# The output projection of a convolution block as three products of rounded and remainder parts, inside a three-layer kernel

## The chip, the cores and the metric

The kernel runs on one core of one Trainium2 chip. The metric is the device time of one launch, in microseconds (us). Engines are named as in the profile: PE is TensorE's matrix multiplication and PEld its weight load, DVE is VectorE, ACT is ScalarE, POOL is GpSimd, SP is SyncE, which here only issues transfers.

## The reference

Three transformer-like layers over 256 tokens of width 1024, all in float32. The middle one is a convolution block, and the change is in its last steps:

```python
def conformer_conv(h, w_in, b_in, dw_w, dw_b, ln_g, ln_b, w_out, b_out):
    val, gate = jnp.split(h @ w_in + b_in, 2, axis=-1)
    u = val * jax.nn.sigmoid(gate)
    u = depthwise_conv_centred(u, dw_w) + dw_b      # 31 taps over the tokens
    u = jax.nn.silu(layer_norm(u, ln_g, ln_b))
    return u @ w_out + b_out                        # w_out is 1024 x 1024
```

A gated feed-forward (`ffn1`) follows it, and then the third layer, which holds a diagonal state-space scan. The scan needs tables that depend on its parameters alone (`a_re`, `a_im`, `log_dt`, `b_re`, `b_im`): exponentials, sines and cosines of angles reduced to one turn. The kernel works them out early, beside the convolution block; this is the scan set-up.

## The kernel before

Everything is kept in SBUF; only weights stream in. They come in chunks through a ring of four slots of 3072 columns (`ring`), in an order fixed in `ORDERED`; SP issues a chunk's load when the last user of the slot's chunk before has signalled. The output weights of the convolution block are four chunks `conf_o` of two 128-row blocks each (2048 columns), so each takes two thirds of a slot. Each engine has its program written out in order; semaphores join them. Activations lie feature by feature: 1024 features are 8 blocks k of 128 partitions, 256 tokens are the columns, in two tiles t of 128.

A float32 product of TensorE is written as one `matmul`, and the trace lists two records for it: the 32 matmuls of `out_rows` are 64 records of line 840. A product of tensors of type fp32r (float32 rounded to what one pass takes) is one record. The feed-forwards already use this: ScalarE rounds each weight block to a high part (`Copy` into fp32r, line 1622), VectorE subtracts it from the weight (low part, line 2221), and TensorE forms high x high, high x low and low x high (lines 894, 895 and 929).

The convolution block, in order:

- TensorE: eight pairs of input products (`glu_pair`, 809), four of the eight channel blocks' convolution as products (`conv_taps`, 1315, and `conv_sum`, 1326, for blocks 4 to 7), the two sums of the layer norm over the features (1350), a broadcast of the gains (`row_bc`, 818), the bias (834), and then `out_rows` (840): for k 0 to 3 both token tiles, for k 4 to 7 first tile 0, then `row_bc(3)`, then tile 1 with four transposes of the next norm (778) in it. After that the first block of `ffn1` (914).
- ScalarE: sigmoid of each gate (`glu_gate`, 1940), copies of what `conv_taps` left in PSUM (`conv_rows`, 1948), `conv_out` (1953), then the squares of the layer norm (1965), a root (1967), eight SiLUs (1970) that write `cout`, and then its part of the scan set-up: two exponentials (1973, 1975) and four sines (1978 to 1982).
- VectorE: `glu_in` (2560) for each block, the 31 taps for blocks 0 to 3 as a chain of 120 `scalar_tensor_tensor` (2574), both of whose tensor inputs lie in SBUF, the layer norm's arithmetic (2587 to 2597), and then the scan set-up (2600 to 2675): `lam_re` ... the two reduced angle arrays `f0`, `f1` (2600 to 2626, its first half) and coefficients and tables (2630 to 2675, its second half). Its end, `bbar_ready`, releases ScalarE to the first rounding for `ffn1`; VectorE goes on with `row_diag(3)` (2185), which TensorE's `row_bc(3)` needs, and with `split` (2221) and `post` (2200 to 2208), the norm and residual after the projection.
- GpSimd: four builds of tap matrices (2936, a `tensor_tensor` of 992 columns) and some clearing, up to 535 us; then nothing until the third layer.

## Time and profile before

| | us |
|---|---|
| median of 3 runs | 1345.48 (1345.28 to 1346.31) |
| span of the profiled execution, first to last instruction | 1342.6 |
| convolution block's projection on TensorE (line 840) | 620.0 to 652.0 |
| busy over the span: PE / DVE / ACT / POOL | 1271.3 / 865.9 / 507.1 / 124.1 |

The profiled execution has no time of its own beside its span in the figures at hand; the median of the runs is 2.9 us above the span. A span counts from the first to the last instruction on the core, so sums over the trace are made against 1342.6 and carried over to 1345.48 with that 2.9 us kept. Times of the trace are in us from the start of the span, durations of single instructions in us or ns as marked.

### The profile page before, as it was taken

The numbers are of one execution on the slowest core, as the hardware profiler recorded it, in microseconds if no ns is written. First come the engines' busy times: TensorE is split into PE (matmuls) and PEld (weight loads), VectorE is DVE, ScalarE is ACT, GpSimd is POOL, SyncE is SP. The second block draws the span as 40 slices with busy tenths as digits, with TensorE's granted clock in tenths as the row PEclk, the third lists the DMA queues.
The fourth block names the chain that finished last, engine by engine and source line by source line (L and its number), as shares of the span: only waits on it lengthen the run. The fifth ranks groups of instructions, "written<-read, shape, count | busy, mean of one in ns | idle before, by whom it ended". The sixth has DMA issues, their size and how long they took to land. (4 is left out here: it accounts for less than half of the span.)

```text
span 1342.6 us, 19019 instructions
## 1 busy us (share of the span) xinstructions
PE 1271.3 (95%) x7198; PEld 985.6 (73%) x7198; DVE 865.9 (64%) x1505; ACT 507.1 (38%) x857; POOL 124.1 (9%) x165
## 2 busy tenths in 40 slices
PE   3999979989999998999999999899999999899997
PEld 1787645554888887874688888687778785688886
DVE  0547886444777775886777776499952432777776
ACT  2664266324544444014644443302123312544443
POOL 0061021000000002000000000255520000000000
PEclk9999989999999998999999999999999999899999
DMA  9322376984655542421555555033324323455551
GB/s 390 128 82 95 134 299 267 386 318 172 218 187 187 189 155 81 148 92 54 190 210 189 188 189 202 33 126 141 141 95 142 112 100 118 161 188 187 188 187 60
DMA packets 24949, 225.78 MB, mean 168 GB/s; under 512 B 2737, under 2 KB 2865, under 8 KB 4658
## 3 DMA queue, kind: packets, MB, share of 16 engines
q1 hardware_dynamic: 23328, 220.31, 45.0%
q10 hardware_dynamic: 1554, 4.56, 1.0%
q8 instruction: 45, 0.74, 0.2%
q14 instruction: 22, 0.18, 0.0%
HBM read 223.81 MB, written 1.05 MB: 167 GB/s over the span
## 5 line engine op out<-in xcount | busy, mean ns | idle before, releaser
L894 PE MATMUL psum<-aT_r,arena_r 128*128 128x512 f32 x920 | 327.7, 398 | 1.5 <-DVE arena_r L2221 1.3
L2221 DVE TENSOR_TENSOR arena_r<-ring,arena_r 128x1024 fp32r<-128x1024 f32 x188 | 220.2, 1220 | 106.5 <-ACT arena_r L1622 106.5
L809 PE MATMUL psum<-aT,ring 128*128 128x256 f32 (+1 forms) x1136 | 265.3, 391 | 0.0
L895 PE MATMUL psum<-aT_r,arena_r 128*128 128x256 f32 x920 | 258.1, 281 | 0.0
L809 PEld LDWEIGHTS psum<-aT,ring 128*128 128x128 f32 x1136 | 214.1, 191 | 45.9 <-issue 18.8
L1622 ACT ACTIVATE arena_r<-ring 128x1024 fp32r<-128x1024 f32 x188 | 186.8, 1051 | 149.8 <-PE psum L929 133.6
L929 PE MATMUL psum<-arena_r 128*128 128x512 f32 x876 | 213.4, 392 | 0.0
L894 PEld LDWEIGHTS psum<-aT_r,arena_r 128*128 128x128 f32 x920 | 172.9, 188 | 44.2 <-issue 2.2
L929 PEld LDWEIGHTS psum<-arena_r 128*128 128x128 f32 x876 | 159.5, 188 | 34.8
L895 PEld LDWEIGHTS psum<-aT_r,arena_r 128*128 128x128 f32 x920 | 173.8, 189 | 2.6
L1634 ACT ACTIVATE nrm<-nrm 128x256 f32<-128x256 f32 x76 | 31.8, 418 | 164.6 <-DVE nrm L2239 161.4
L792 PE MATMUL psum<-ring,cond 128*32 128x384 f32 x512 | 53.7, 545 | 24.7 <-DMA consts<-in_consts 12.7
L2574 DVE SCALAR_TENSOR_TENSOR arena<-arena,cols 128x256 f32<-128x256 f32 x120 | 52.8, 481 | 1.9
L792 PEld LDWEIGHTS psum<-ring,cond 128*32 128x32 f32 x512 | 14.7, 116 | 52.5 <-issue 35.1
L2239 DVE TENSOR_REDUCE nrm<-psum 128x256 f32<-128x512 f32 x73 | 49.8, 682 | 0.0
L2256 DVE TENSOR_TENSOR nrm<-nrm 128x256 f32<-128x256 f32 x76 | 32.3, 426 | 21.7 <-ACT nrm L1634 16.3
L2246 DVE TENSOR_REDUCE nrm<-psum 128x256 f32<-128x512 f32 x42 | 29.0, 691 | 20.8 <-PE psum L895 20.8
L2346 DVE SCALAR_TENSOR_TENSOR arena<-arena,cols 128x512 f32<-128x512 f32 (+1 forms) x48 | 35.3, 763 | 1.1
L2012 ACT ACTIVATE arena<-psum,cols 128x256 f32<-128x256 f32 x24 | 11.4, 473 | 58.2 <-PE psum L809 58.2
L2264 DVE TENSOR_TENSOR arena_r<-nrm,arena_r 128x256 fp32r<-128x256 f32 x73 | 31.1, 425 | 2.5
L840 PE MATMUL psum<-ring,yT 128*128 128x512 f32 x64 | 28.3, 595 | 2.3 <-DVE o L2522 1.4
L1513 PE MATMUL psum<-yT,ring 128*128 128x256 f32 x128 | 29.0, 380 | 0.9 <-DVE yT L2816 0.9
(499 smaller groups left out, 1620.7 us busy)
## 6 DMA issues: line engine op xcount, KB each, us to landing
ring<-in_w_ffn SPq DMA_DIRECT2D x44, 1536.0 KB, 6.6
ring<-in_w_mod SPq DMA_DIRECT2D x32, 1536.0 KB, 8.9
ring<-in_w_ff SPq DMA_DIRECT2D x32, 1024.0 KB, 4.9
ring<-in_w_in_g SPq DMA_DIRECT2D x8, 1536.0 KB, 6.4
ring<-in_w_conf_i SPq DMA_DIRECT2D x8, 1024.0 KB, 4.9
ring<-in_w_hyb_f SPq DMA_DIRECT2D x4, 1536.0 KB, 6.5
ring<-in_w_in_a SPq DMA_DIRECT2D x4, 1536.0 KB, 6.4
ring<-in_w_in_b SPq DMA_DIRECT2D x4, 1536.0 KB, 6.8
```

Of the source, the lines that this page charges most:

```text
L792: last = mm(mod_acc[q:q + 32, :], cond[:, at:at + 32], slot(c)[:, k * MOD_C:(k + 1) * MOD_C], start=(m == m0 and k < 4), stop=(m == m1 - 1 ...
L809: last = mm(bank(use)[:, out_at:out_at + rhs(k).shape[1]], weights[:, k * P:(k + 1) * P], rhs(k), start=(k == 0), stop=(k == KT - 1))
L894: mm(bank(use).rearrange("p (a t) -> p a t", a=2), hi, x_both[:, :, k, :], start=(k == 0), stop=False)
L895: last = mm(bank(use)[:, T:2 * T], lo, x_hi[:, k, :], start=False, stop=(k == KT - 1))
L929: last = mm(Y[:, t, half * 512:half * 512 + 512], act_part, w_part[:, half * 512:half * 512 + 512], start=(isinstance(i, int) and j == 0 a ...
L1622: fn(out_hi[2] if last_out else w_hi[j % 2][:, at], slot(c)[:, at], ACT.Copy).then_inc(split_hi, 1)
L1634: fn(sg[:, j % 2, :], g_sum[:, j % 2, :], func).then_inc(act_on, 1)
L2221: tt(lo, slot(c)[:, at], hi.bitcast(F32), ALU.subtract).then_inc(split_ready, 1)
L2239: summed = v.reduce_sum(g_sum[:, j % 2, :], bank(gate).rearrange("p (a t) -> p t a", a=2), axis=AXX)
L2256: tt(h_tmp, sg[:, j % 2, :], u_sum if parts == 3 else sg[:, j % 2, :], ALU.mult).then_inc(h_step, 1)
L2346: last = stt(cv[:, b, 0:n, :], cin[:, b, 0:n, k:k + T], taps[:, b, k:k + 1], cv[:, b, 0:n, :], ALU.mult, ALU.add)
L2574: last = stt(cc[:, c, :], cu[:, c, k:k + T], dww[:, c, k:k + 1], cc[:, c, :], ALU.mult, ALU.add)
```

## The change

The output projection of the convolution block becomes three fp32r products for each one in float32: `out_rows_parts` takes the place of `out_rows`. For it

- ScalarE rounds the eight weight blocks (`conf_weights`, a `Copy` of 128x1024) between its `glu_gate`, `conv_rows` and `conv_out` steps; the high parts go to the free third of the ring slots and to four other free places;
- GpSimd subtracts each high part from its weight block, in place in the ring (eight `tensor_tensor` of 128x1024, both inputs in SBUF), each as soon as its rounding is done;
- after each SiLU ScalarE rounds `cout` (`conf_round`, 128x256) and VectorE makes the low part (`conf_part`, a subtraction of 128x256);
- the first half of the scan set-up moves: on VectorE from behind the layer norm to ahead of it, on ScalarE the two exponentials and four sines from behind the SiLUs to between the `conv_out` steps and ahead of the squares.

```diff
--- before.py
+++ after.py
@@ -443,6 +443,10 @@
             s = SLOT_OF[c]
             return ring[:, s * SLOT:(s + 1) * SLOT]
+        def out_weights(c, kk, t=None):
+            at = SLOT_OF[c] * SLOT + kk * D
+            return (ring if t is None else t)[:, at:at + D]
+
         def part_of(n, t):
             name, j, at, width = HYB_PARTS[n]
@@ -555,7 +559,11 @@
         taps = [x[:, at:at + D] for x in (yT_t, ybuf_t) for at in (0, D)]
         conv_ev = [view(x, 0, 4, T + 3) for x in (nrm_t, decay_t)]
         Y_quads = psum[:, 2048:4096].rearrange("p (g n) -> p g n", g=4)[:, :, 0:T + 3]
-        cout = csq
+        cout, cout_hi, cout_lo = csq, view(arena_r, 0, KT, T), view(arena_r, 4352, KT, T)
+        spare = [ring_r[:, s * SLOT + 2 * D:s * SLOT + 3 * D] for s in range(SLOTS)]
+        spare = [spare[SLOT_OF[FIRST["conf_o"] + c]] for c in range(4)]
+        conf_o_hi = [spare[0], o_r[:, 0:D], spare[1], arena_r[:, 7168:7168 + D], spare[2], z_r[:, 0:D], spare[3],
+                     arena_r[:, 11264:11264 + D]]
         ring_ready = [sem(f"ring_ready{s}") for s in range(SLOTS)]
@@ -603,6 +611,7 @@
         taps_ready = sem("taps_ready")
         csig_ready, conv31, csq_ready, csq_done = sem("csig_ready"), sem("conv31"), sem("csq_ready"), sem("csq_done")
         ln_sd, ln_x, conf_out = sem("ln_sd"), sem("ln_x"), sem("conf_out")
+        conf_hi, conf_lo, conf_w_hi, conf_w_lo = sem("conf_hi"), sem("conf_lo"), sem("conf_w_hi"), sem("conf_w_lo")
         s5_par, s5_mag, s5_arg, s5_trig = sem("s5_par"), sem("s5_mag"), sem("s5_arg"), sem("s5_trig")
         bbar_ready, logf_in, logf_sp, logf_ready = sem("bbar_ready"), sem("logf_in"), sem("logf_sp"), sem("logf_ready")
         cdiag_ready, s5_tab, masked = sem("cdiag_ready"), sem("s5_tab"), sem("masked")
@@ -622,7 +631,7 @@
         small_trig = view(arena, 14376, 2, S5T, 32)
         glu = view(arena, 15400, 4, P)
         bbd = view(arena, 13352, 2, 4, P)
-        trig_tmp = view(arena, 8232, 6, 512)
+        trig_tmp = view(arena, 8192, 6, 512)
         cdiag = view(arena, 11304, 2, 512)
         y_a, y_b = yT[:, 0:4, :], yT[:, 4:8, :]
         mT = view(tok_t, 0, KT, T)
@@ -865,6 +874,47 @@
                                 norm_tile(p + 2, 0)
                         if t and c == 2:
                             last.then_inc(ring_used, 1)
+                    if t == 0:
+                        last.then_inc(y_first, 1)
+                        row_bc(p + 1)
+                    else:
+                        filled(last, USE["y", p][0])
+
+            def out_rows_parts(c0, p, hi, lo, w_hi_of, act_ready, w_ready, bias=False):
+
+                wait_y(p)
+                if bias:
+                    for t in range(TT):
+                        for half in range(2):
+                            mm(Y[:, t, half * 512:half * 512 + 512], ones[0:1, :],
+                               brow[0:1, half * 512:half * 512 + 512], start=True, stop=False)
+
+                def rows_of(k, t):
+                    w_lo_k = out_weights(c0 + k // 2, k % 2, ring_r)
+                    for n, (act_part, w_part) in enumerate(((hi, w_hi_of[k]), (hi, w_lo_k), (lo, w_hi_of[k]))):
+                        for half in range(2):
+                            last = mm(Y[:, t, half * 512:half * 512 + 512], act_part[:, k, t * P:(t + 1) * P],
+                                      w_part[:, half * 512:half * 512 + 512],
+                                      start=(k == 0 and n == 0 and not bias), stop=(k == KT - 1 and n == 2))
+                    return last
+
+                for k in range(4):
+                    act_ready(k)
+                    w_ready(k)
+                    for t in range(TT):
+                        last = rows_of(k, t)
+                    if k % 2:
+                        last.then_inc(ring_used, 1)
+                for t in range(TT):
+                    for k in range(4, KT):
+                        if t == 0:
+                            act_ready(k)
+                            w_ready(k)
+                        last = rows_of(k, t)
+                        if t and k == 5:
+                            last.then_inc(ring_used, 1)
+                        if t and k == 6:
+                            norm_tile(p + 2, 0)
                     if t == 0:
                         last.then_inc(y_first, 1)
                         row_bc(p + 1)
@@ -1351,7 +1401,8 @@
                 filled(last, use)
             row_bc(2)
             pe.wait_ge(brow_loaded, 16)
-            out_rows(FIRST["conf_o"], cout, 2, lambda k: pe.wait_ge(conf_out, k + 1), True)
+            out_rows_parts(FIRST["conf_o"], 2, cout_hi, cout_lo, conf_o_hi, lambda k: pe.wait_ge(conf_lo, k + 1),
+                           lambda k: pe.wait_ge(conf_w_lo, k + 1), True)
             ffn("ffn1", NF, 3)
@@ -1952,27 +2003,32 @@
                 wait_full(act, use)
                 freed(fn(cc[:, c, :], bank(use)[:, 0:T], ACT.Identity, bias=col("conf_dw_b")[:, c:c + 1]), use)
+            def conf_weights(k):
+
+                c = FIRST["conf_o"] + k // 2
+                act.wait_ge(ring_ready[SLOT_OF[c]], 16 * (TURN_OF[c] + 1))
+                fn(conf_o_hi[k], out_weights(c, k % 2), ACT.Copy).then_inc(conf_w_hi, 1)
+
             for c in range(7):
                 glu_gate(c)
+            for k in range(2):
+                conf_weights(k)
             conv_rows(0)
+            for k in range(2, 6):
+                conf_weights(k)
             glu_gate(7)
-            for n in range(1, len(CONV_PE)):
-                conv_rows(n)
-                conv_out(n - 1)
-            conv_out(len(CONV_PE) - 1)
-            for k in range(KT):
-                act.wait_ge(ln_x, k + 1)
-                fn(csq[:, k, :], cc[:, k, :], ACT.Square).then_inc(csq_done, 1)
-            wait_read(act, USE["ln"][1])
-            fn(crs, crs, ACT.Sqrt).then_inc(ln_sd, 1)
-            for k in range(KT):
-                act.wait_ge(csq_ready, k + 1)
-                fn(cout[:, k, :], csq[:, k, :], ACT.Silu, scale=col("conf_ln_g")[:, k:k + 1],
-                   bias=col("conf_ln_b")[:, k:k + 1]).then_inc(conf_out, 1)
-
+            conv_rows(1)
+            conv_out(0)
+            for k in range(6, KT):
+                conf_weights(k)
+            conv_rows(2)
+            conv_out(1)
             fn(dt, col("log_dt"), ACT.Exp).then_inc(s5_mag, 1)
+            conv_rows(3)
             act.wait_ge(s5_par, 1)
             fn(mag, s5_a, ACT.Exp).then_inc(s5_mag, 1)
+            conv_out(2)
+            conv_out(3)
             act.wait_ge(half_ready, 1)
             act.wait_ge(s5_arg, 1)
             fn(sin_h, phi, ACT.Sin, scale=PI).then_inc(s5_trig, 1)
@@ -1980,6 +2036,24 @@
             act.wait_ge(s5_arg, 2)
             fn(trig_tmp[:, 2, :], trig_tmp[:, 0, :], ACT.Sin, scale=PI).then_inc(s5_trig, 1)
             fn(trig_tmp[:, 3, :], trig_tmp[:, 1, :], ACT.Sin, scale=-PI, bias=halfpi[:, :]).then_inc(s5_trig, 1)
+
+            for k in range(KT):
+                act.wait_ge(ln_x, k + 1)
+                fn(csq[:, k, :], cc[:, k, :], ACT.Square).then_inc(csq_done, 1)
+            wait_read(act, USE["ln"][1])
+            fn(crs, crs, ACT.Sqrt).then_inc(ln_sd, 1)
+
+            def conf_round(k):
+                act.wait_ge(conf_out, k + 1)
+                fn(cout_hi[:, k, :], cout[:, k, :], ACT.Copy).then_inc(conf_hi, 1)
+
+            for k in range(KT):
+                act.wait_ge(csq_ready, k + 1)
+                fn(cout[:, k, :], csq[:, k, :], ACT.Silu, scale=col("conf_ln_g")[:, k:k + 1],
+                   bias=col("conf_ln_b")[:, k:k + 1]).then_inc(conf_out, 1)
+                if k:
+                    conf_round(k - 1)
+            conf_round(KT - 1)
             row_copy(2)
             act.wait_ge(bbar_ready, 1)
             split("ffn1", 0, [2])
@@ -2582,20 +2656,6 @@
                             glu_in(c)
                             break
-            use = USE["ln"][0]
-            wait_full(dve, use)
-            freed(ts(crs, bank(use)[:, 0:T], 1.0 / D, None, ALU.mult), use)
-            wait_read(dve, use)
-            for k in range(KT):
-                tt(cc[:, k, :], cc[:, k, :], crs, ALU.subtract).then_inc(ln_x, 1)
-            use = USE["ln"][1]
-            wait_full(dve, use)
-            freed(mean_eps(crs, bank(use)[:, 0:T], D), use)
-            dve.wait_ge(ln_sd, 1)
-            ch(v.reciprocal(crs, crs))
-            for k in range(KT):
-                tt(csq[:, k, :], cc[:, k, :], crs, ALU.mult).then_inc(csq_ready, 1)
-
             dve.wait_ge(s5_mag, 1)
             ch(ts(lam_re, col("a_re"), -1e-4, None, ALU.min))
             ch.mark(tt(theta, col("a_im"), dt, ALU.mult))
@@ -2624,6 +2684,31 @@
             ch(tt(f0, f0, f5, ALU.subtract))
             ch(tt(f0, f0, f4, ALU.add))
             stt(f1, f0, -1.0, f0, ALU.mult, ALU.max).then_inc(s5_arg, 1)
+
+            use = USE["ln"][0]
+            wait_full(dve, use)
+            freed(ts(crs, bank(use)[:, 0:T], 1.0 / D, None, ALU.mult), use)
+            wait_read(dve, use)
+            for k in range(KT):
+                tt(cc[:, k, :], cc[:, k, :], crs, ALU.subtract).then_inc(ln_x, 1)
+            use = USE["ln"][1]
+            wait_full(dve, use)
+            freed(mean_eps(crs, bank(use)[:, 0:T], D), use)
+            dve.wait_ge(ln_sd, 1)
+            ch(v.reciprocal(crs, crs))
+
+            def conf_part(k):
+
+                dve.wait_ge(conf_hi, k + 1)
+                tt(cout_lo[:, k, :], cout[:, k, :], cout_hi[:, k, :].bitcast(F32), ALU.subtract).then_inc(conf_lo, 1)
+
+            for k in range(KT):
+                tt(csq[:, k, :], cc[:, k, :], crs, ALU.mult).then_inc(csq_ready, 1)
+                if k == 5:
+                    conf_part(0)
+
+            for k in range(1, KT):
+                conf_part(k)
             dve.wait_ge(s5_trig, 2)
             dve.wait_ge(s5_mag, 2)
@@ -2942,6 +3027,12 @@
             ch.sync()
             gp.memset(tick[:, :], 0.0).then_inc(margins, 1)
+            for k in range(KT):
+                pool.wait_ge(conf_w_hi, k + 1)
+                c = FIRST["conf_o"] + k // 2
+                tt(out_weights(c, k % 2, ring_r), out_weights(c, k % 2), conf_o_hi[k].bitcast(F32),
+                   ALU.subtract).then_inc(conf_w_lo, 1)
+
             pool.wait_ge(norm_x, 24)
             ch.mark(gp.memset(cin2[:, :, 0:2], 0.0))
             ch.sync()
```

`conf_weights(k)` stands on ScalarE as: gates 0 to 6, weights 0 and 1, `conv_rows(0)`, weights 2 to 5, gate 7, `conv_rows(1)`, `conv_out(0)`, weights 6 and 7, `conv_rows(2)`, `conv_out(1)`, exponential, `conv_rows(3)`, exponential, `conv_out(2)`, `conv_out(3)`, four sines.

## Rows read from the trace of the kernel before

**Rows 1.** The page: busy time, share of the span, instructions.

```profile
PE 1271.3 (95%) x7198; PEld 985.6 (73%) x7198; DVE 865.9 (64%) x1505; ACT 507.1 (38%) x857; POOL 124.1 (9%) x165
```

**Rows 2.** Timeline of PE: start, us, engine, line, operation, count [idle before <-releaser].

```profile
603.15 1.91 PE L1326 MATMUL psum<-decay,consts 128*32 128x256 f32 x32
605.86 3.69 PE L1350 MATMUL psum<-arena,consts 128*128 128x256 f32 x16 [0.80 <-ACT arena L1953]
611.07 3.69 PE L1350 MATMUL psum<-arena,consts 128*128 128x256 f32 x16 [1.51 <-ACT arena L1965]
614.60 1.88 PE L818 MATMUL psum<-diag,consts 128*128 128x512 f32 x4
...
620.03 22.55 PE L840 MATMUL psum<-ring,arena 128*128 128x512 f32 x48
642.42 1.88 PE L818 MATMUL psum<-diag,consts 128*128 128x512 f32 x4
644.13 5.31 PE L840 MATMUL psum<-ring,arena 128*128 128x512 f32 x12
```

**Rows 3.** Timeline of DVE, the end of the taps, the norm, the set-up.

```profile
587.17 0.48 DVE L2560 SCALAR_TENSOR_TENSOR arena<-psum,cols,arena 128x256 f32<-128x256 f32 x1 [1.78 <-ACT arena L1940]
587.57 14.62 DVE L2574 SCALAR_TENSOR_TENSOR arena<-arena,cols 128x256 f32<-128x256 f32 x32
609.59 0.42 DVE L2587 TENSOR_SCALAR arena<-psum 128x256 f32<-128x256 f32 x1 [7.40 <-PE psum L1350]
...
617.49 2.77 DVE L2597 TENSOR_TENSOR arena<-arena 128x256 f32<-128x256 f32 x8
623.55 0.17 DVE L2600 TENSOR_SCALAR arena<-cols 128x16 f32<-128x16 f32 x1 [3.29 <-ACT arena L1973]
...
629.55 0.69 DVE L2626 SCALAR_TENSOR_TENSOR arena<-arena 128x512 f32<-128x512 f32 x1
...
637.46 1.22 DVE L2185 TENSOR_TENSOR diag<-consts,pcol 128x1024 f32<-128x1024 f32 x1
```

**Rows 4.** Timeline of ACT, places where it is free, and a sine.

```profile
575.86 0.47 ACT L1940 ACTIVATE arena<-psum,cols 128x256 f32<-128x256 f32 x1 [6.43 <-PE psum L809]
579.59 1.03 ACT L1948 ACTIVATE nrm<-psum 128x1036 f32<-128x1036 f32 x1 [3.26 <-PE psum L1315]
...
605.13 0.47 ACT L1953 ACTIVATE arena<-psum,cols 128x256 f32<-128x256 f32 x1 [1.25 <-PE psum L1326]
...
630.27 0.63 ACT L1981 ACTIVATE arena<-arena 128x512 f32<-128x512 f32 x1 [2.59 <-DVE arena L2626]
```

**Rows 5.** The page: a rounding of 128x1024 on ACT.

```profile
L1622 ACT ACTIVATE arena_r<-ring 128x1024 fp32r<-128x1024 f32 x188 | 186.8, 1051 | 149.8 <-PE psum L929 133.6
```

**Rows 6.** Timeline of SP's queue: the loads of conf_o.

```profile
562.04 24.95 SPq L694 DMA_DIRECT2D ring<-in_w_conf_o  x4
```

**Rows 7.** The chain that ended last: three-product rows in a feed-forward.

```profile
1229.19 2.78 PE psum L929 x12
```

**Rows 8.** Timeline of POOL while it builds tap matrices.

```profile
525.23 1.86 POOL L2936 TENSOR_TENSOR yT<-sel,cols 128x992 f32<-128x992 f32 x1
...
527.10 1.86 POOL L2936 TENSOR_TENSOR yT<-sel,cols 128x992 f32<-128x992 f32 x1
...
528.98 2.78 POOL L2936 TENSOR_TENSOR ybuf<-sel,cols 128x992 f32<-128x992 f32 x1
```

**Rows 9.** Timeline of DVE at the same time.

```profile
527.29 2.75 DVE L2185 TENSOR_TENSOR diag<-consts,pcol 128x1024 f32<-128x1024 f32 x1
```

**Rows 10.** That line and the taps of line 2346: duration ns min/median/max.

```profile
L2185 DVE TENSOR_TENSOR diag<-consts,pcol x6: 1217/1222/2748, 230.7 to 1117.5; 128x1024 f32<-128x1024 f32 x6
...
L2346 DVE SCALAR_TENSOR_TENSOR arena<-arena,cols x48: 477/752/1941, 90.2 to 193.3; 128x512 f32<-128x512 f32 x32, 128x256 f32<-128x256 f32 x16
```

**Rows 11.** Timeline of DVE: taps of another layer beside POOL.

```profile
90.25 6.03 DVE L2346 SCALAR_TENSOR_TENSOR arena<-arena,cols 128x512 f32<-128x512 f32 x4
```

**Rows 12.** Timeline of POOL beside those taps.

```profile
91.56 0.90 POOL L2887 TENSOR_TENSOR ring<-ring,rows 128x128 f32<-128x128 f32 x1
92.55 1.90 POOL L2891 TENSOR_TENSOR ring<-ring,consts 128x640 f32<-128x640 f32 x1
```

**Rows 13.** Windows: busy time of PE, PEld, DVE, ACT, POOL, then granted clock.

```profile
621.00:623.00 2.00, 2.00 (x4) 0.92 (x3) 0.00 (x0) 1.98 (x4) 0.00 (x0) 0.50 0.00 0
```

## The prediction

> **What bounds the kernel now.** I read the page first: TensorE is busy for 95% of the span [rows 1], so what counts is time taken from TensorE or waits added to it. Then the timelines of the four engines between 575 and 660 us, the stretch that the change touches, to see who waits for whom there. TensorE ends the channel products at 605.06 (603.15 + 1.91), sums for the layer norm at 605.86 and at 611.07, and from there works without a pause: gains, bias, and the projection from 620.03 [rows 2]. VectorE is idle for 7.4 us before the norm's first instruction at 609.59, because it ended its taps at 602.19 (587.57 + 14.62); it does the scan set-up from 623.55 to 637.4, in the shadow of the projection [rows 3]. So three things set when the projection ends: when VectorE can start the norm (609.59), the chain from there to TensorE's start (10.44 us), and the products. Last I looked at how GpSimd and VectorE behave when both work, because the change puts eight large GpSimd instructions beside the taps.
>
> **The products.** The float32 form: 48 records in 22.39 us up to the start of `row_bc(3)` at 642.42, then 12 records from 644.13 in 5.15 us, 0.429 each [rows 2] (5.15 and not 5.31, since the next instruction starts before the last record ends). 48 at 0.429 would be 20.6; the missing 1.8 us are the clock, granted at 0.50, the lower of its two levels, at 621 to 623 [rows 13], after TensorE's pauses around 605 and 610. The new form has for each (k, t) the same six matmuls as a feed-forward's output rows, 12 of which advance the chain by 2.78 us, 0.232 each [rows 7]. Up to `row_bc(3)` there are 8 pairs for k 0 to 3 and 4 for tile 0: 72 matmuls, 16.7 us in place of 22.39, a gain of **5.7 us** if the clock is at its upper level there. Tile 1 has 24, 5.6 us in place of 16 records at 0.429, 6.9: a gain of 1.3, of which I take **1.0**, since the transposes among them wait for VectorE's norm of tile 0, which gets no faster.
>
> **The start of the projection, taken alone.** SiLU, then rounding, then a subtraction come ahead of the first product. VectorE's norm products begin at 617.49, one per about 0.35 us (8 in 2.77) [rows 3]; the first low part comes behind six of them and costs one more, so it is done at about 620.0, just when TensorE has done the bias. Later blocks need about 0.9 us each on ScalarE (a SiLU and a Copy) and TensorE takes 2.8 us for a block's both tiles, so they are not late. Cost: 0. Without the cover of the bias it would be 1.5 us.
>
> **The roundings of the weights.** Eight Copies at 1.05 us on ScalarE [rows 5]. The loads of `conf_o` are issued from 562.0 to 587.0 [rows 6]. Blocks 0 and 1 fit behind the gate that starts at 575.86 and before `conv_rows(0)` at 579.59 [rows 4]; 2 to 5 between there and the gate that now serves VectorE at 587.17 [rows 3]; the last two after 592.7, when the fourth chunk is in. ScalarE's idle time hides them, cost 0; without it, 8.4 us.
>
> **The moved set-up.** Its first half lasts from 623.55 to 630.24 on VectorE (629.55 + 0.69), 6.7 us [rows 3]. It goes into the 7.4 us of idle time ahead of 609.59, so alone it costs nothing, with 0.7 us to spare. ScalarE's second exponential now waits for VectorE's first set-up values, and `conv_out(2)` and `conv_out(3)` stand behind it, and TensorE's first norm sum behind those: harmless while VectorE ends its taps at 602.2, since `conv_out(3)` can't run before 605.13 anyway [rows 4], but if VectorE is late, they are late with it. The two large sines stand ahead of the squares; they can start only at the end of the half. One is 0.63 us [rows 4]; when the half ends just as the norm starts, they put the first square off by some 0.2. The second half of the set-up (to `row_diag(3)` at 637.46) follows the low parts: 7.2 us after about 15.8 us of norm and parts, so `row_diag(3)` is done some 24 us and the weights' split some 26 us after the norm's start, and tile 0 of the projection ends after 10.5 + 16.7 = 27.2. It is covered, by 1 us for the split.
>
> **GpSimd's subtractions, the disputed part.** Eight `tensor_tensor` of 128x1024 with both inputs in SBUF. The nearest row is one of 992 columns, 1.86 us undisturbed [rows 8], so 1.92 for 1024. The first six are due from 577.4 to 584.5, the last two at about 594, all while VectorE runs its taps, each with two SBUF inputs. What happens then is in three places of the trace. `row_diag` of 1024 columns usually takes 1.22 us [rows 10]; started 0.19 us into a GpSimd `tensor_tensor`, it takes 2.75 [rows 9], 1.53 more, and GpSimd's next one takes 2.78 in place of 1.86 [rows 8]. Four taps of 512 columns, 0.75 each when alone [rows 10], take 6.03 [rows 11], about 3.2 too long, and the GpSimd instructions beside them are long too (a 640-column one 1.90, a 128-column one 0.90) [rows 12]. The two engines take turns, a whole instruction each. Per instruction VectorE loses 1.53 + 0.19 = 1.72 of GpSimd's 1.86; for 1024 columns 1.77. Eight make **14.2 us**, less the 1.78 us that VectorE idled for the gate at 587.17 [rows 3]: the taps end at 602.2 + 12.4 = 614.6. Bounds: at 1.5 us each +10.2, at 2.1 us each +15.0. The Trainium skill (GPSIMD Engine Reference, section Elementwise — side-by-side cycle accounting) gives 4.5 us for a GpSimd add of 2048 columns; that would be an estimated 2.2 us for 1024, and the sum would be about 3 us higher. The trace's 1.86 for 992 speaks against it, though its inputs repeat elements; no row shows two plain inputs of this size.
>
> The Trainium skill (SBUF — State Buffer, section Who interferes with whom) goes a little further than these rows: an instruction of VectorE with two SBUF inputs and one of GpSimd that reads SBUF exclude each other for the whole instruction. By it the price would be 1.92 each, 15.4 in all, and the time 1352.
>
> What is late next: set-up half to 614.6 + 6.7 = 621.3. The second exponential at about 615, two `conv_out` (0.47 each) to 616.1, then TensorE's first sum of 3.7 us; after a pause of 8 to 9 us its clock is likely at the lower level, so it ends at 620 to 622. The norm starts at about 621.5 in place of 609.59: **+11.9**. I add 0.2 for the sines.
>
> **The sum.** +11.9 + 0.2 - 5.7 - 1.0 = **+5.4 us**: span 1348.0, and with the 2.9 us outside it 1350.9, in round numbers 1351.
>
> **The rivals.**
> - *The engines don't get in each other's way here* (or GpSimd yields): the half fits the idle time, and 5.7 + 1.0 are gained, less nothing: 1345.5 - 6.7 = 1338.8. The point from which it decides: the change gains while the taps end before 602.2 + 0.7 + 6.7 = 609.6, that is while VectorE loses under (7.4 + 1.78) / 8 = 1.15 us to each GpSimd instruction. For it: the taps are of 256 columns, unlike any pair in the trace. Against: each of the three places shows whole turns, and 1.15 is under two thirds of 1.86. Chance 0.08.
> - *The loss about equals the gain:* GpSimd takes 0.9 to 1.4 us of VectorE per instruction, or VectorE catches up elsewhere; 1343 to 1348. Chance 0.09.
> - *The forecast,* 1348.3 to 1354. Chance 0.73.
> - *Dearer still:* GpSimd at 2.2 us on plain inputs (+3), or the lower clock again in the norm's second sum and at the projection's start (+1.8 as before): 1354 to 1358. Chance 0.08.
> - *Three products gain nothing over the float32 form,* so that the whole 12.1 stays: 1357.6. The rows of the feed-forward speak clearly against it. Chance 0.02.
>
> **How the numbers follow.** What a measurement of this kernel can tell from no change is about 0.2%, 2.7 us. Slower by more (over 1348.2): the forecast, the dearer case and the one that gains nothing, 0.83. Within: 0.09. Faster by more: 0.08. The range leaves out the first rival and most of the second below, and the last above: 1347 to 1355.5.
>
> **What would show it.** In the changed profile: taps of line 2574 (its new number) of 0.48 us with pauses or lengths of about 2 us wherever a GpSimd `tensor_tensor` of 1024 runs, and the last one ending near 614.6; the norm's first instruction at about 621.5, released by TensorE or following the set-up directly; TensorE idle for some 8 us before its first norm sum; 72 matmuls of the projection in about 16.7 us; no pause of TensorE between bias and projection. The forecast is wrong if the taps still end near 602, if GpSimd's instructions last much under 1.8 us, or if the norm's start is late by less than 7 us.

## The result, and the profile after

The changed kernel takes 1357.08 us (median of 4 runs, 1356.12 to 1357.83), the kernel before 1345.88 beside it (4 runs, 1345.28 to 1346.31): a ratio of 1.0078, 95% interval 1.0065 to 1.0091. It is slower by 11.2 us, where 5.4 were forecast, and 1.6 us above the range. The profiled execution took 1357.83 us, 1.8 more than its span of 1356.0.

The page of the changed kernel, busy time, share of the span and instructions, against [rows 1]: TensorE is no busier, VectorE by 19.5 us, GpSimd by 20.2.

```profile
PE 1271.8 (94%) x7230; PEld 995.4 (73%) x7230; DVE 885.4 (65%) x1513; ACT 516.9 (38%) x873; POOL 144.3 (11%) x173
```

Times of the two traces can't be set side by side as they stand, since this execution is already 2.8 us later when the stretch begins: the gate of block 6 starts at 578.64, in before at 575.86 [rows 4], and no edit bears on what runs before it. So I count from that gate.

First the timeline of GpSimd in the changed kernel (start, us, engine, line, operation): its eight subtractions.

```profile
580.13 2.65 POOL L3033 TENSOR_TENSOR ring_r<-ring,ring_r 128x1024 fp32r<-128x1024 f32 x1 [43.28 <-ACT ring_r L2010]
...
592.76 2.55 POOL L3033 TENSOR_TENSOR ring_r<-ring,z_r 128x1024 fp32r<-128x1024 f32 x1
596.54 2.35 POOL L3033 TENSOR_TENSOR ring_r<-ring,ring_r 128x1024 fp32r<-128x1024 f32 x1 [1.23 <-ACT ring_r L2010]
598.86 2.52 POOL L3033 TENSOR_TENSOR ring_r<-ring,arena_r 128x1024 fp32r<-128x1024 f32 x1
```

Seven of the eight last 2.5 to 2.65 us, and the one at 596.54, which had waited for its weights, 2.35; 1.92 was forecast. Now the timeline of VectorE over the same time, against [rows 3].

```profile
585.50 0.47 DVE L2634 SCALAR_TENSOR_TENSOR arena<-psum,cols,arena 128x256 f32<-128x256 f32 x1
585.90 18.51 DVE L2648 SCALAR_TENSOR_TENSOR arena<-arena,cols 128x256 f32<-128x256 f32 x14
604.32 0.48 DVE L2634 SCALAR_TENSOR_TENSOR arena<-psum,cols,arena 128x256 f32<-128x256 f32 x1
604.72 14.62 DVE L2648 SCALAR_TENSOR_TENSOR arena<-arena,cols 128x256 f32<-128x256 f32 x32
619.26 0.17 DVE L2660 TENSOR_SCALAR arena<-cols 128x16 f32<-128x16 f32 x1
...
625.25 0.69 DVE L2686 SCALAR_TENSOR_TENSOR arena<-arena 128x512 f32<-128x512 f32 x1
627.59 0.42 DVE L2690 TENSOR_SCALAR arena<-psum 128x256 f32<-128x256 f32 x1 [1.64 <-PE psum L1400]
```

The 14 taps from 585.90 take 18.51 us, the later 32, with no GpSimd beside them, 14.62 as before. The line's own view (duration in ns, min/median/max) shows what happened in between:

```profile
L2648 DVE SCALAR_TENSOR_TENSOR arena<-arena,cols x120: 476/480/2628, 545.8 to 618.9; 128x256 f32<-128x256 f32 x120
```

Half of the taps take 480 ns or less, and the longest 2628: one waits for a whole GpSimd instruction. All 120 sum to 69.0 us where they were 52.8, so each subtraction took (69.0 - 52.8) / 8 = 2.03 us from VectorE. The taps end at 619.26 and not at 602.19; the set-up's half runs until 625.94, and the norm starts at 627.59 instead of 609.59 [rows 3]: 48.95 us after the gate instead of 33.73, **+15.2**. What the norm waited for at the end was TensorE. ScalarE's timeline against [rows 4]:

```profile
608.65 0.47 ACT L2004 ACTIVATE arena<-psum,cols 128x256 f32<-128x256 f32 x1 [8.87 <-PE psum L1376]
...
619.76 0.21 ACT L2029 ACTIVATE arena<-arena 128x16 f32<-128x16 f32 x1 [5.75 <-DVE arena L2662]
619.88 0.82 ACT L2004 ACTIVATE arena<-psum,cols 128x256 f32<-128x256 f32 x2
```

Its second exponential waits 5.75 us for VectorE's first set-up values, and the last two `conv_out` stand behind it. TensorE's timeline against [rows 2] (the projection is line 896, the bias 889, the norm's sums 1400):

```profile
604.95 3.64 PE L1376 MATMUL psum<-decay,consts 128*32 128x256 f32 x32 [6.27 <-DVE arena L2634]
...
614.57 1.91 PE L1376 MATMUL psum<-decay,consts 128*32 128x256 f32 x32
620.95 6.60 PE L1400 MATMUL psum<-arena,consts 128*128 128x256 f32 x16 [4.47 <-ACT arena L2004]
629.07 3.69 PE L1400 MATMUL psum<-arena,consts 128*128 128x256 f32 x16 [1.51 <-ACT arena L2042]
...
634.40 4.58 PE L889 MATMUL psum<-tok,consts 1*128 1x512 f32 x8
638.91 5.32 PE L896 MATMUL psum<-ring_r,arena_r 128*128 128x512 f32 x12
...
657.68 1.88 PE L827 MATMUL psum<-diag,consts 128*128 128x512 f32 x4
...
665.92 3.73 PE L964 MATMUL psum<-yT,ring 128*128 128x128 f32 x32
```

There are two pauses, and I had seen one. At 604.95 `conv_sum(1)` has waited 6.27 us for `glu_in(7)` of VectorE, which stood behind the long taps (604.32 above). At 620.95 the first norm sum has waited 4.47 us for `conv_out`. What follows each is slow: 3.64 us for 32 instructions that otherwise take 1.91, and 6.60 for a sum of 3.69. The bias takes 4.58, and the projection's first 12 matmuls 5.32, where 12 at the prediction's 0.232 would be 2.8. The bias in before took 3.70:

```profile
616.41 3.70 PE L834 MATMUL psum<-tok,consts 1*128 1x512 f32 x8
```

The windows view (busy time of PE, PEld, DVE, ACT, POOL, then the granted clock) says why these are slow:

```profile
603.00:605.00 2.00, 0.05 (x4) 0.08 (x8) 1.97 (x6) 0.00 (x0) 0.00 (x0) 0.50 0.00 0
621.00:623.00 2.00, 2.00 (x5) 1.65 (x6) 1.90 (x7) 1.31 (x2) 0.00 (x0) 0.50 0.00 0
629.00:631.00 2.00, 1.93 (x9) 1.76 (x10) 1.82 (x6) 2.00 (x7) 0.00 (x0) 1.00 0.00 0
639.00:641.00 2.00, 2.00 (x5) 1.61 (x6) 1.25 (x3) 2.00 (x6) 0.00 (x0) 0.50 0.00 0
```

The clock is at 0.50 of full speed, 1.2 GHz, in the first, second and fourth of these, and at 2.4 GHz in the third. Slices of 1 and 2 us over the whole stretch show three such times of about 6.8 us (from some 603, 620 and 637); before had one of about half that length [rows 13]. The first two begin inside the pauses, some 4.3 us after TensorE stopped at 598.7 and 3.5 us after it stopped at 616.5; the third begins with TensorE at work since 629.07. The 72 matmuls take 638.91 to 657.68, 18.77 us.

The sum, from the gate: norm start +15.2; from there to the projection 11.32 us instead of 10.44, +0.9; the 72 matmuls 18.77 instead of 22.39, -3.6; from `row_bc(3)` to the next block 8.24 instead of 9.46, -1.2; the start of `ffn1`'s products -0.5. Together +10.8 by the two profiles, and the medians say +11.2. In the forecast's sum, then, the norm's +11.9 came out as +15.2 and the -5.7 of the 72 matmuls as -3.6.

### The profile page after: what moved, and what is told of

The parts are those of the page before. It is cut to its first block and busy times, and to the rows that moved or that the text cites. A ratio compares the mean times of both kernels' runs of the same rounds, so it can differ in the third digit from the quotient of the medians.

```text
span 1356.0 us, 19119 instructions
## 1 busy us (share of the span) xinstructions
PE 1271.8 (94%) x7230; PEld 995.4 (73%) x7230; DVE 885.4 (65%) x1513; ACT 516.9 (38%) x873; POOL 144.3 (11%) x173
## 5 line engine op out<-in xcount | busy, mean ns | idle before, releaser
L818 PEld LDWEIGHTS psum<-aT,ring 128*128 128x128 f32 x1136 | 214.9, 191 | 45.8 <-issue 18.8
L2648 DVE SCALAR_TENSOR_TENSOR arena<-arena,cols 128x256 f32<-128x256 f32 x120 | 69.0, 617 | 1.9
```

Of the source, the lines that this page charges most:

```text
L818: last = mm(bank(use)[:, out_at:out_at + rhs(k).shape[1]], weights[:, k * P:(k + 1) * P], rhs(k), start=(k == 0), stop=(k == KT - 1))
L2648: last = stt(cc[:, c, :], cu[:, c, k:k + T], dww[:, c, k:k + 1], cc[:, c, :], ALU.mult, ALU.add)
```

## The experiments

Theory and rivals. *Sharing:* GpSimd's subtractions hold VectorE off its taps, and all that is slower follows from the late norm, TensorE's lower clock after its pauses included. *Rivals:* the roundings, the moved set-up or the products themselves cost it. The table has all runs: times in us, the ratio to before with its interval, and from each profile the time from the gate of block 6 to the norm's first instruction, to the projection's first, to `row_bc(3)` and to `ffn1`'s first split product. Before ran again beside all of them (medians 1345.97 to 1346.6), and the ratios are to those runs.

| kernel | median (runs) | ratio | norm | proj. | bc(3) | ffn1 |
|---|---|---|---|---|---|---|
| before | 1345.88 (4) | 1 | 33.7 | 44.2 | 66.6 | 88.6 |
| changed | 1357.08 (4) | 1.0078 [1.0065, 1.0091] | 49.0 | 60.3 | 79.0 | 99.4 |
| 1 no subtraction | 1339.38 (5) | 0.9954 [0.9941, 0.9967] | 33.8 | 44.2 | 62.2 | 82.6 |
| 2 before + subtractions | 1355.29 (5) | 1.0068 [1.0053, 1.0082] | 42.1 | 53.9 | 76.6 | 98.6 |
| 3 set-up back | 1352.69 (5) | 1.0052 [1.0038, 1.0066] | 42.3 | 54.0 | 74.0 | 95.9 |
| 4 TensorE kept busy | 1353.01 (6) | 1.0051 [1.0035, 1.0068] | 47.2 | 58.0 | 76.0 | 96.4 |
| 5 GpSimd writes only | 1338.95 (6) | 0.9952 [0.9936, 0.9968] | 33.8 | 44.2 | 62.3 | 82.6 |
| 6 subtraction alone | 1346.39 (10) | 1.0001 [0.9988, 1.0014] | 33.8 | 44.3 | 66.7 | 88.5 |
| 7 on VectorE | 1348.43 (12) | 1.0015 [1.0003, 1.0027] | 42.9 | 53.3 | 69.8 | 90.5 |
| 8 set-up early | 1346.93 (12) | 1.0007 [0.9997, 1.0016] | 38.6 | 51.3 | 69.4 | 89.8 |
| 9 all in idle time | 1338.77 (6) | 0.9951 [0.9933, 0.9968] | 33.8 | 44.2 | 62.3 | 82.6 |

**1. No subtraction.** GpSimd clears one column in place of each subtraction, and TensorE takes the high part of the weights where it took the low one (the weights' low parts are left out; the number of matmuls is the same).

```diff
-                    w_lo_k = out_weights(c0 + k // 2, k % 2, ring_r)
+                    w_lo_k = w_hi_of[k]
-                tt(out_weights(c, k % 2, ring_r), out_weights(c, k % 2), conf_o_hi[k].bitcast(F32),
-                   ALU.subtract).then_inc(conf_w_lo, 1)
+                gp.memset(out_weights(c, k % 2)[:, 0:1], 0.0).then_inc(conf_w_lo, 1)
```

> The changed kernel, but GpSimd clears one column in place of each of its eight subtractions of 128x1024, and TensorE takes the high part of the weights where it took the low one (the low part of the weights is left out; the number and shape of the matmuls stay). Theory, turns between GpSimd and VectorE: the taps end near 602 to 605 us, the norm starts 18 us earlier than in the changed kernel, and the time is about 1339 (1337 to 1341), 6.7 under the kernel before. Rival, the moved set-up or the roundings on ScalarE cost the time: the time stays above 1350.

1339.38 us, 17.7 below the changed kernel. The page's row of the taps, and TensorE's first norm sum and `row_bc(3)`:

```profile
L2648 DVE SCALAR_TENSOR_TENSOR arena<-arena,cols 128x256 f32<-128x256 f32 x120 | 52.8, 482 | 1.9
```

```profile
605.38 3.69 PE L1400 MATMUL psum<-arena,consts 128*128 128x256 f32 x16 [0.80 <-ACT arena L2004]
...
637.60 1.88 PE L827 MATMUL psum<-diag,consts 128*128 128x512 f32 x4
```

The taps are back at 52.8 us, the sum at 3.69, the norm at its old place. Roundings and the moved half of the set-up are hidden, as the prediction had it; the rivals that blame them fall. Everything that the change loses hangs on the eight subtractions, directly or through what they delay.

**2. Before, with the subtractions added.** Eight plain subtractions of 128x1024 into a free place, each when its weights are in; TensorE's projection otherwise untouched.

```diff
+            for k in range(KT):
+                c = FIRST["conf_o"] + k // 2
+                pool.wait_ge(ring_ready[SLOT_OF[c]], 16 * (TURN_OF[c] + 1))
...
+                x, y = slot(c)[:, 0:D], slot(c)[:, D:2 * D]
+                tt(arena_r[:, 7168:7168 + D], (x, y)[k % 2], (y, x)[k % 2], ALU.subtract).then_inc(probe, 1)
```

> The kernel before with one thing added: eight GpSimd subtractions of 128x1024 of two halves of a loaded output-weight chunk into an unused place, each as soon as its chunk is in, all beside the taps. Theory, turns: each takes about 2.0 us from VectorE, the taps end 14 us later, the norm starts some 8 to 10 us later, the time is 1354 to 1357. Rival, GpSimd runs beside VectorE for nothing and something else in the change costs the time: 1346.

1355.29 us, 9 us slower with nothing else changed but one wait of TensorE ahead of the projection, for subtractions that had long ended. GpSimd's timeline (x2 and x4 are two and four instructions in the time given):

```profile
567.55 5.05 POOL L2953 TENSOR_TENSOR arena_r<-ring 128x1024 fp32r<-128x1024 f32 x2 [32.30 <-DMA ring<-in_w_conf_o]
576.61 10.03 POOL L2953 TENSOR_TENSOR arena_r<-ring 128x1024 fp32r<-128x1024 f32 x4 [4.01 <-DMA ring<-in_w_conf_o]
592.44 4.97 POOL L2953 TENSOR_TENSOR arena_r<-ring 128x1024 fp32r<-128x1024 f32 x2 [5.80 <-DMA ring<-in_w_conf_o]
```

Some 2.5 us each; the taps take 69.1 us, as in the changed kernel. The float32 projection suffers from the clock too, here in the bias (841 is the projection):

```profile
625.48 5.04 PE L835 MATMUL psum<-tok,consts 1*128 1x512 f32 x8
630.45 22.87 PE L841 MATMUL psum<-ring,arena 128*128 128x512 f32 x48
```

**3. The half of the set-up put back behind the norm,** on both engines, the subtractions as in the changed kernel.

> The changed kernel with the moved half of the set-up back behind the norm and the low parts, on VectorE and ScalarE. Theory, turns: the taps end as late as in the changed kernel, the norm starts about 7 us earlier, but 14 us of set-up then end after tile 0 of the projection and hold it and the next block some 4 us: 1352 to 1355. Rival, the move is what costs: the time returns to 1346 or below.

1352.69 us. Without the set-up ahead of it the norm starts 42.3 us after the gate and not 49.0: the moved half, free in experiment 1, costs 6.6 us once the taps are late. Part of that is TensorE's: its first norm sum, 6.60 us in the changed kernel, takes 3.69 here. Behind the norm it has a price too, since it holds up `row_diag(3)`:

```profile
649.67 1.98 PE L827 MATMUL psum<-diag,consts 128*128 128x512 f32 x4 [1.32 <-DVE diag L2259]
```

TensorE idles 1.32 us for VectorE's `diag`. The net of moving the half is a loss of 4.4 us by the medians, 3.5 by the profiles.

**4. TensorE kept busy through its pauses.** Extra float32 matmuls, whose result is overwritten, six ahead of `conv_sum(1)` and five behind the last channel sum.

```diff
+            def keep_busy(n):
+                for _ in range(n):
+                    mm(bank(USE["ln"][0]), ones, consts[:, 0:512], start=True, stop=True)
...
+                    keep_busy(6)
...
+            keep_busy(5)
```

> The changed kernel with eleven idle float32 products of 128x512 on TensorE (six ahead of conv_sum(1), five behind conv_sum(3)), in its two pauses, into a free PSUM bank. Theory, part of the excess over the forecast is TensorE's lower clock after the pauses: the first norm sum takes 3.7 in place of 6.6 us, bias and the projection's first matmuls lose 3 us less, the time is 1352 to 1354. Rival, the lower clock is hidden or of no weight: 1356 to 1358.

1353.01 us, 4.1 below the changed kernel by the medians and 3.0 by the profiles (96.4 against 99.4).

```profile
618.85 3.69 PE L1408 MATMUL psum<-arena,consts 128*128 128x256 f32 x16 [2.28 <-ACT arena L2012]
...
630.90 3.69 PE L889 MATMUL psum<-tok,consts 1*128 1x512 f32 x8
```

Sum and bias are at 3.69 again. The norm starts 1.7 us sooner, the way to the projection is 0.5 shorter and the 72 matmuls take 18.0 us instead of 18.8. These 3.0 us are the part of the loss that the clock carries after the pauses, and more work on the engine in its idle time won it back.

**5. GpSimd writes only.** As experiment 1, but GpSimd clears all 1024 columns of each block.

```diff
-                gp.memset(out_weights(c, k % 2)[:, 0:1], 0.0).then_inc(conf_w_lo, 1)
+                gp.memset(out_weights(c, k % 2)[:, :], 0.0).then_inc(conf_w_lo, 1)
```

> As the run with one cleared column, but each of the eight GpSimd instructions clears all 1024 columns: it writes SBUF and reads none (the low part of the weights is left out; the matmuls stay in number and shape). If the engines take turns only where GpSimd reads: as that run, 1339, VectorE's taps of 0.48 us each. If a write takes the turn as well, at about 0.95 us each: 7.6 us less the idle time of 2.5, 1343 to 1345.

```profile
L3033 POOL MEMSET ring<- x8: 951/951/952, 576.0 to 593.4; 128x1024 f32 x8
```

```profile
L2648 DVE SCALAR_TENSOR_TENSOR arena<-arena,cols 128x256 f32<-128x256 f32 x120 | 52.8, 481 | 1.9
```

Eight instructions of 0.95 us beside the taps, and the taps don't notice: 52.8 us. So it is not GpSimd's writing that shuts VectorE out. That its reading does is what is left; these instructions are also shorter and of another kind, and a read alone was not run.

**6. A plain subtraction alone.** Before, with two such GpSimd instructions at 537 us, where VectorE has almost nothing to do.

> The kernel before with two plain GpSimd subtractions of 128x1024 (two different stretches of SBUF as inputs, fp32r out) right behind the tap matrices, at about 535 us, where VectorE waits for a gate. It measures such an instruction by itself: 1.9 us by the row that the forecast took, 2.07 by the taps' lengthening in the changed kernel, 2.5 if its length there was its own. The time does not change, 1346.

```profile
L2948 POOL TENSOR_TENSOR arena_r<-consts x2: 2344/2348/2353, 537.0 to 539.4; 128x1024 fp32r<-128x1024 f32 x2
```

2.35 us each, with nobody beside them but one `glu_in` of VectorE (0.48 us, from 537.92); none of the three expected values. The same page has 1857 ns for the tap builds of 992 columns, as before [rows 8]. So the difference of 0.49 us is not the sharing; the instruction itself is dearer than the one that I took its price from. The tap build repeats elements of its inputs, but it also multiplies, and two groups of GpSimd in the trace of before speak for the operation as the cause:

```profile
L2873 POOL TENSOR_TENSOR ring<-tok x2: 1247/1416/1585, 75.3 to 76.8; 128x640 f32<-128x640 f32 x2
```

```profile
L2976 POOL TENSOR_TENSOR ybuf<-ybuf,consts x2: 1264/1266/1268, 992.5 to 1005.4; 128x512 f32<-128x512 f32 x2
```

The first multiplies without repeated elements, and the shorter of the two, with VectorE idle, takes 1247 ns for 640 columns: 1.95 ns a column, no more than the tap build's 1.87. The second subtracts, with VectorE idle as well, and takes 1266 for 512: 2.47 a column, although one input is repeated; the plain subtraction has 2.29. No run changes the operation alone, so this is not shown, but rows for a better price were there: twice the 1266 is an estimate of 2.5 us for 1024 columns.

**7. The weight subtractions on VectorE,** all eight between the taps and the half of the set-up.

```diff
+            for k in range(KT):
+                conf_w_part(k)
```

> The changed kernel with the eight subtractions of the weights on VectorE, between the last tap and the moved half of the set-up, and none on GpSimd. Theory, turns: the taps end at about 602 again; then 8 x 1.14 = 9.2 us of subtractions and 6.7 us of set-up, so the norm starts near 618.5 in place of 627.6 (2.8 us of which came ahead of this stage), with TensorE's clock low after the longer pause: 1350 to 1353. Rival, the loss in the changed kernel is only the instructions' own length and it does not matter which engine has them: 1356 to 1358.

1348.43 us, below the 1350 to 1353 that were expected. VectorE takes 1.14 us for each, little more than half of what one cost it on GpSimd. TensorE:

```profile
615.95 5.82 PE L1400 MATMUL psum<-arena,consts 128*128 128x256 f32 x16 [7.82 <-ACT arena L2004]
...
632.24 3.04 PE L896 MATMUL psum<-ring_r,arena_r 128*128 128x512 f32 x12
...
648.72 1.88 PE L827 MATMUL psum<-diag,consts 128*128 128x512 f32 x4
```

The pause ahead of the norm sum is now one of 7.82 us, the sum takes 5.82, but the lower clock is over before the projection: its 72 matmuls take 16.48 us (632.24 to 648.72). That is the only run here that shows the forecast's 16.7. The norm starts 42.9 us after the gate, as expected (the expected 618.5 less before's gate at 575.86 is 42.6), so what came out shorter than expected lies behind it.

**8. The whole set-up ahead of the taps,** the subtractions on VectorE, four behind the taps and four behind the activations' parts.

> A version made from the findings: the three products, nothing on GpSimd, all of the scan set-up ahead of the taps, where VectorE waits for the first gates, four of the eight weight subtractions on VectorE between the last tap and the norm, four behind the low parts of the activations. Theory: the norm starts at 609.6 to 611, where it did before, the products' gain is kept, 1338 to 1342. Rival, the earlier set-up delays the first gates and the taps by more than the idle time has room for: above 1345.

1346.93 us, 5 us above the range that was expected (1338 to 1342), and the rival's case. VectorE and ScalarE at the start of the convolution block:

```profile
537.04 0.17 DVE L2640 TENSOR_SCALAR arena<-cols 128x16 f32<-128x16 f32 x1 [4.67 <-POOL tick L3039]
...
554.92 0.73 DVE L2721 TENSOR_SCALAR arena<-arena,cols 128x256 f32<-128x256 f32 x2
```

```profile
545.02 1.28 ACT L1991 ACT_TABLE_LOAD   x1
546.31 0.84 ACT L1991 ACTIVATE arena<-psum,cols 128x256 f32<-128x256 f32 x2
```

The set-up can begin only when GpSimd has done its tap matrices and clearing (4.67 us idle before 537.04), the sines and their table loads stand ahead of ScalarE's first gate, which comes at 546.31, and the taps begin 23.8 us before the gate of block 6, where before they begin 33.6 before it. They end 7.8 us later from that gate than in before, and the four subtractions behind them take another 4.5: together 4.9 more than the 7.4 us that VectorE idled, which is how late the norm is. TensorE, which has its first norm sum ready, pauses for 5.13 us meanwhile, and its second sum takes 5.98 us, so the way from the norm to the projection is 12.7 us and not 10.4. I had taken the idle time there as free for all of it; one half fits, and only with the sines elsewhere.

**9. Each piece where its engine idles.** The half of the set-up on VectorE between `glu_in(0)` and `glu_in(1)`, only the first exponential ahead of ScalarE's gates, six subtractions between the last tap and the norm, one behind the norm's products, one behind the activations' parts. GpSimd has none.

```diff
+            glu_in(1)
...
+            for k in range(6):
+                conf_w_part(k)
+
             use = USE["ln"][0]
...
+            conf_w_part(6)
...
+            conf_w_part(7)
```

> The three products stay; GpSimd has no part in them. VectorE makes the eight low parts of the weights itself: six between its last tap and the norm (6 x 1.14 = 6.8 us, in the 7 us that it idles there), one behind the norm's eight products, one behind the low parts of the activations. The first half of the scan set-up (6.7 us) stands between glu_in(0) and glu_in(1), where VectorE idles some 6 us and GpSimd has ended its tap matrices; of ScalarE's set-up work the first exponential stands ahead of its first gate, the rest where the changed kernel has it. Theory (only a late start of the norm and TensorE's lower clock after long pauses cost the changed kernel its gain; where VectorE's work fits its idle time, the products' gain of 6.7 us is kept): taps of 52.8 us ending at about 602.5, norm's first instruction at 609.3 to 610.5, TensorE's norm sums of 3.69 us, 1339 to 1341. Rival (as in the run with the whole set-up ahead of the taps: exponential and set-up early push gates and taps back): taps end at 605 or later, norm at 612 or later, 1344 to 1348. Rival two (the pieces behind the norm's products hold back the last blocks' products): norm at 610 but a pause of TensorE of over 1 us inside the projection, 1341 to 1343.

1338.77 us (6 runs, 1335.83 to 1341.4), ratio 0.9951 [0.9933, 0.9968]: 7.2 us faster than before in the runs beside it (1345.97) and 18.3 faster than the changed kernel, just under the 1339 to 1341 that the theory expected. VectorE and TensorE:

```profile
602.35 1.22 DVE L2692 TENSOR_TENSOR ring_r<-ring,ring_r 128x1024 fp32r<-128x1024 f32 x1
...
608.03 1.22 DVE L2692 TENSOR_TENSOR ring_r<-ring,z_r 128x1024 fp32r<-128x1024 f32 x1
609.84 0.42 DVE L2700 TENSOR_SCALAR arena<-psum 128x256 f32<-128x256 f32 x1 [0.59 <-PE psum L1400]
```

```profile
606.11 3.69 PE L1400 MATMUL psum<-arena,consts 128*128 128x256 f32 x16 [0.80 <-ACT arena L2004]
...
620.28 4.61 PE L896 MATMUL psum<-ring_r,arena_r 128*128 128x512 f32 x12
...
638.34 1.88 PE L827 MATMUL psum<-diag,consts 128*128 128x512 f32 x4
```

Six subtractions fill the wait from 602.35 on, and the norm starts 0.59 us after the last of them. TensorE has no long pause. Still the 72 matmuls take 18.06 us, and the windows view shows the lower clock near their start, as in before [rows 13]:

```profile
621.00:623.00 2.00, 2.00 (x6) 1.53 (x5) 1.22 (x4) 2.00 (x6) 0.00 (x0) 0.50 0.00 0
```

## Why the prediction was right in direction and too low

**What held.** TensorE's waits decide; the products gain; roundings and start of the projection are hidden (1); a tap waits for a whole subtraction of GpSimd (the 2628 ns tap, and 2); VectorE is late, and with it the second exponential, `conv_out` and the first sum. The sum without the sharing, 1338.8, was the first rival, and kernels 1, 5 and 9 measured 1339.4, 1339.0 and 1338.8. That is partly luck: by the profiles the 72 matmuls gain 4.3 us in kernel 9 and not 5.7, and what follows them 1.7 and not 1.0.

**The first step that failed: 14.2 us for the subtractions.** The step "so 1.92 for 1024" took the price of a subtraction from an instruction that multiplies, with repeated inputs. The subtraction takes 2.35 (6) and costs VectorE 2.03, not 1.77; that is 86% of its length, where the forecast had 92%. Eight make 16.2; less the 1.78 that VectorE idled anyway, the taps end 14.3 us late from the gate instead of 12.4: 1.9 us. The Trainium skill (GPSIMD Engine Reference, section Elementwise — side-by-side cycle accounting) has 4.5 us for 2048 columns, from which I had estimated 2.2 and set it aside; the measured 2.35 is nearer to it than to the row. Its sum, 3 us higher, would have been 1354. The Trainium skill (SBUF — State Buffer, section Who interferes with whom) says that the conflict is with GpSimd's reads and not with an instruction that only writes; experiment 5 agrees, at 52.8 us for the taps.

**The second step that failed: TensorE's clock.** The forecast took it as low once, inside the first sum, and gave that sum a guess of "620 to 622" and the products "if the clock is at its upper level". Three terms were short by it: the way from the taps' end to the norm, 8.3 us instead of 6.9 (+1.4); the way to the projection (+0.9, of which 0.2 were booked for the sines); the 72 matmuls, 18.8 instead of 16.7 (+2.1). Experiment 4 undoes 3.0 us of this. The rest is the products' 1.3 us, which no lateness explains: kernels 1, 4, 5, 8 and 9 all have 18.0 to 18.1 us, with the clock low at the projection's start, and only 7, where it is high from 621 on, has 16.5. I had seen that window in before [rows 13], charged it to the old form and not to the new.

Together 1.9 + 1.4 + 0.7 + 2.1 = 6.1 us, against 0.2 and 0.5 that the tail and `ffn1` gave back: +5.4 becomes +10.8. Each of the two is in the prediction as part of the rival "dearer still", but as alternatives, with 0.08 together; the measured time lies in that rival's range. They came both, and the second follows from the lateness that the forecast itself had worked out: a pause of 8 us was written down, and what it would do to the engine afterwards was priced in one place of three. A pause that was not seen at all, TensorE's 6.27 us for `glu_in(7)`, belongs to the same omission: of VectorE's late steps I followed only the last.

**Left open.** Why the clock falls at the start of the projection even without a long pause (9) is not told by these runs: 4 shows only that it does so also when the earlier pauses are filled, and the changed kernel and 7, both low at their first norm sum, differ in it. The 2.8 us between the profiles ahead of the gate are from stages that the change doesn't touch.

## What to carry to other kernels

Work is hidden only while its cover stands: the moved half of the set-up cost nothing behind taps that ended on time (1) and 6.6 us behind late ones (3), so a plan with two edits has to be costed with both in. An idle engine is no free place for work whose reads collide with the busy engine's; here VectorE did each subtraction itself in 1.14 us, against the 2.03 us that it lost to GpSimd's, and eight such pieces placed where it waited anyway turned a loss of 11 us into a gain of 7, with the set-up's half moved into idle time as well. A row that prices an instruction should match it in its operation too, and not only in its columns. Where a forecast holds a pause of TensorE, the rows after it are to be priced at the lower clock too.

## What the runs showed of the hardware

- A GpSimd subtraction of 128x1024 from plain float32 inputs into fp32r takes 2.35 us alone and 2.52 to 2.65 beside VectorE's taps; a multiplication of 992 columns whose inputs repeat elements takes 1.86. By columns alone the subtraction would be 1.92.
- Beside taps with two SBUF inputs, GpSimd's subtractions come every 2.5 us, and one tap is done for each, where alone one is done every 0.46 us; with writes alone (8 times 0.95 us) the taps keep their 52.8 us.
- In the changed kernel TensorE's granted clock fell to 0.50 inside each of its two long pauses, 4.3 and 3.5 us after they began, and stayed there for some 6.8 us. At the projection's start it fell for as long once more, and for about half of that in before and in kernels 1 and 9, which had no such pause. Eleven useless float32 matmuls in the pauses made the kernel 3 to 4 us faster.
